# A two-block model kernel on one core: key norms found once, one VectorE operation per state update, decays read one step back

## What is computed

```
kk = heads(k * k_k);  kk = kk * rsqrt(max(sum(kk * kk, per head), 1e-12))
kd = k * (1 + (a - 1) * k_a)                  # a = sigmoid(...), for each direction
S  = S * w_t + (S @ -kk_t) x (kk_t * a_t) + v_t x kd_t      # one step of the scan
y_t = S @ r_t
yn = (y - mean) * rsqrt(var + eps) * lnx_g + lnx_b;  bonus = sum(r * kd * r_k) * v
out = (yn + bonus) * gate
```

## Time and profile before

| | us |
|---|---|
| median of 3 runs | 4076.07 (4070.96 to 4079.86) |
| the profiled execution, its own time | 4080.79 |
| its span in the trace | 4079.0 |
| PE busy | 3704.1 (91%) |
| DVE busy | 2383.0 (58%) |
| ACT busy | 1628.4 (40%) |

### The profile page before, as it was taken

The page is one execution under the profiler, slowest core; times in us unless marked ns, Lnnn a source line. Parts: engine busy times, 40 slices in busy tenths (PEclk is TensorE's granted clock), DMA queues, the critical chain, the costliest instruction groups (busy, mean ns, idle before and its releaser), DMA issues.

```text
span 4079.0 us, 82585 instructions
## 1 busy us (share of the span) xinstructions
PE 3704.1 (91%) x33100; PEld 3370.1 (83%) x33100; DVE 2383.0 (58%) x4281; ACT 1628.4 (40%) x2283; POOL 24.3 (1%) x47
## 2 busy tenths in 40 slices
PE   7999998989899999995999877777778989999998
PEld 5998877779899999994889546666666989999998
DVE  4759995655577775444435437766665444444443
ACT  4545553223455554333123333333231345555333
POOL 0000000000000000000000000000000000000000
PEclk9999998989999999997999987877777999999999
DMA  4547663445355555551234540000000535555553
GB/s 158 175 155 260 248 264 136 155 156 175 134 178 183 184 185 173 181 182 69 93 103 154 189 162 4 5 6 5 5 5 3 185 134 185 185 175 185 179 181 114
DMA packets 80711, 572.00 MB, mean 140 GB/s; under 512 B 9488, under 2 KB 9744, under 8 KB 15472
## 3 DMA queue, kind: packets, MB, share of 16 engines
q1 hardware_dynamic: 78048, 558.50, 39.2%
q0 software_dynamic: 2448, 10.46, 0.8%
HBM read 566.82 MB, written 2.10 MB: 139 GB/s over the span
## 4 chain that ended last, share of the span: by engine, by line
PE 76%; DVE 17%; issue 3%; DMA 2%; ACT 1%; DVEq 0%; SPq 0%; ACTq 0%; POOL 0%
PE po L254 17%; PE po L255 17%; PE po L256 17%; PE po L1424 6%; DVE w_lo L242 2%; PE pa L989 2%; PE po L989 1%; PE pa L300 1%; PE po L418 1%; DMA raw<-ada 1%; DVE s_v L680 1%; PE pa L897 1%; PE po L468 1%; DVE hf L311 1%; PE po L469 1%
## 5 line engine op out<-in xcount | busy, mean ns | idle before, releaser
L242 DVE TENSOR_TENSOR w_lo<-raw,w_hi 128x1024 fp32r<-128x1024 f32 x880 | 1040.5, 1201 | 460.4 <-ACT w_hi L235 443.6
L235 ACT ACTIVATE w_hi<-raw 128x1024 fp32r<-128x1024 f32 (+1 forms) x877 | 898.1, 1038 | 800.8 <-PE po L256 578.3
L254 PE MATMUL po<-hh,w_lo 128*128 128x256 f32 x3744 | 1065.5, 285 | 24.4 <-DVE hh L335 12.6
L255 PE MATMUL po<-hh,w_hi 128*128 128x256 f32 x3744 | 1061.9, 284 | 0.0
L256 PE MATMUL po<-hh,w_hi 128*128 128x256 f32 x3744 | 1061.8, 284 | 0.0
L254 PEld LDWEIGHTS po<-hh,w_lo 128*128 128x128 f32 x3744 | 721.3, 193 | 29.2 <-issue 28.6
L255 PEld LDWEIGHTS po<-hh,w_hi 128*128 128x128 f32 x3744 | 721.4, 193 | 0.3
L256 PEld LDWEIGHTS po<-hh,w_hi 128*128 128x128 f32 x3744 | 721.2, 193 | 0.0
L254 PE MATMUL po<-f_hi,w_lo 128*128 128x256 f32 x1408 | 399.4, 284 | 6.1 <-DVE f_lo L1652 6.1
L255 PE MATMUL po<-f_lo,w_hi 128*128 128x256 f32 x1408 | 399.2, 284 | 0.0
L256 PE MATMUL po<-f_hi,w_hi 128*128 128x256 f32 x1408 | 399.1, 283 | 0.0
(11 more groups left out here) (544 smaller groups left out, 6554.1 us busy)
## 6 DMA issues: line engine op xcount, KB each, us to landing
raw<-ffn_up SPq DMA_DIRECT2D x176, 1024.0 KB, 4.9
raw<-w_in SPq DMA_DIRECT2D x112, 1024.0 KB, 4.9
raw<-ada SPq DMA_DIRECT2D x96, 1024.0 KB, 6.1
raw<-ffn_down SPq DMA_DIRECT2D x64, 1024.0 KB, 4.9
raw<-w_out SPq DMA_DIRECT2D x32, 1024.0 KB, 4.9
raw<-ffn_down SPq DMA_DIRECT2D x32, 768.0 KB, 4.2
raw<-glu SPq DMA_DIRECT2D x16, 1024.0 KB, 6.8
raw<-dn_proj SPq DMA_DIRECT2D x8, 1024.0 KB, 5.3
```

Source lines behind the costliest of these rows:

```text
L235: act.activation(w_hi[:, k % 4, 0:width], raw[:, k // 2 % ring, (k % 2) * PW:(k % 2) * PW + width], ACT.Copy).then_inc(hi_ready, 1)
L242: dve.tensor_tensor(w_lo[:, k % 4, 0:width], raw[:, k // 2 % ring, (k % 2) * PW:(k % 2) * PW + width], w_hi[:, k % 4, 0:width].bitcast(F32 ...
L254: pe.matmul(po[bank][:, 0:T], lo, act_hi[:, t, :], start=first and n == 0, stop=False)
L255: pe.matmul(po[bank][:, 0:T], hi, act_lo[:, t, :], start=False, stop=False)
```

## The change

The inverse of the chunk matrices stays as it is. Six things are edited.

1. Key norms. The per-tile chain for the norm (two DVE operations, matmul with `k_bd`, bound, root, reciprocal, product) goes. Instead, under the last rounds of `w_in2`, ACT squares all keys (eight 128x512 operations), PE sums them with 16 matmuls into rows of one bank (`under_q_pe`), and one bound, one root and one reciprocal of 32x256 are done. In a prep, step 8 spreads two rows over the partitions by one matmul with `k_pick` (filled by ACT in step 1), and one DVE operation makes the keys from it. `first_keys_dve` shrinks in the same way, and clears two banks.
2. State update. `d` is made of four 64x64 blocks on the diagonal instead of two 64x128 matmuls, so that nothing has to be masked; `ks` moves to the other half of the bank. ACT scales the old state into `k_sg` ahead of time, and one DVE operation gives the new state.
3. Shifted decays. `k_gp` (a DVE subtraction and an ACT exponential for each direction) goes; `k_ah` is made from `k_g` one position back, with a small copy for the chunk's edge.
4. `k_vs` and the factor of `kd` move from DVE to ACT (Copy and Identity).
5. The bonus is one addition and one product instead of two products and one addition.
6. In `post`, three DVE operations after the reciprocal become two.

The core of the diff (names of semaphore steps and tile addresses are left out):

```diff
+        NORM_AT = {7 + 2 * j: j for j in range(8)}
+
         def under_q_pe(pe):
             for s in range(32):
+                if s in NORM_AT:
+                    j = NORM_AT[s]
...
+                    pe.wait_ge(*sqa.at(j, "sq"))
+                    for n in range(2):
+                        m = 16 * n + 2 * j
+                        mm = pe.matmul(pa[2][0:32, 0:T], n_sel[:, 32 - m:64 - m], n_sqs[:, j % 2, n * T:n * T + T],
+                                       start=j == 0 and n == 0, stop=j == 7 and n == 1)
+                    mm.then_inc(sqp.did("sum"), 1)
...
         def under_q_act(act):
...
+                    act.activation(n_sqs[:, j % 2, :], zk[:, j, :], ACT.Square, scale=pcol("k_k", j))\
+                       .then_inc(sqa.did("sq"), 1)
+                if s == 25:
+                    act.wait_ge(rows_eps, 1)
+                    act.activation(n_rows[0:32], n_rows[0:32], ACT.Sqrt).then_inc(rows_sqrt, 1)
...
         def under_q_dve(dve):
...
+                    dve.tensor_scalar(n_rows[0:32], pa[2][0:32, 0:T], 1e-12, None, ALU.max).then_inc(rows_eps, 1)
+                if s == 27:
+                    dve.wait_ge(rows_sqrt, 1)
+                    dve.reciprocal(n_rows[0:32], n_rows[0:32]).then_inc(rows_rec, 1)
...
         def prep_pe(pe, j, x, q):
...
-            pe.matmul(I[2][:, 0:T], k_bd[:], k_nrm[:], start=True, stop=True).then_inc(Q.did("sum"), 1)
+            pe.wait_ge(*A.at(j, "pk"))
+            pe.matmul(I[2][:, 0:T], k_pick[0:32], k_rows[0:32], start=True, stop=True).then_inc(Q.did("sum"), 1)
...
         def prep_act(act, j, x, q):
+            act.activation(k_vs[:], zv[:, ds(j, 1), cols_of(x)].rearrange("p a t -> p (a t)"), ACT.Copy)
...
+                    if n:
+                        act.wait_ge(*A.at(j, f"a{e}"))
+                        settle(act)
+                        act.activation(k_kd[e][:], k_a[e][:], ACT.Identity, bias=k_oka[:, ds(j, 1)],
+                                       scale=par[:, ds(j + COL["k_a"], 1)]).then_inc(A.did(f"t{e}"), 1)
+            norm_pick(act, j * 2 + (16 if x == "c" else 2)).then_inc(A.did("pk"), 1)
...
-                act.activation(k_gp[e][:], k_gp[e][:], ACT.Exp, scale=-DECAY).then_inc(A.did(f"gp{e}"), 1)
...
-            act.wait_ge(*V.at(j, "eps"))
-            act.activation(k_nrm[:], k_nrm[:], ACT.Sqrt).then_inc(A.did("sqrt"), 1)
...
         def prep_dve(dve, j, x, q):
-            signal(dve.tensor_copy(k_vs[:], tile(zv)), "vs")
...
-                then(dve.tensor_tensor_scan(b, k_rst[:], s, 0.0, ALU.mult, ALU.add), f"cs{e}")
-                signal(dve.tensor_tensor(k_gp[e][:], k_cs[e][:], k_s[e][:], ALU.subtract), f"sm{e}")
-                dve.wait_ge(*A.at(j, f"a{e}"))
-                then(dve.tensor_scalar(k_kd[e][:], k_a[e][:], 1.0, scale("k_a"), ALU.subtract, ALU.mult), f"t{e}")
-                then(dve.scalar_tensor_tensor(k_kd[e][:], k_kd[e][:], 1.0, tile(zk), ALU.add, ALU.mult), f"kd{e}")
+                signal(dve.tensor_tensor_scan(b, k_rst[:], s, 0.0, ALU.mult, ALU.add), f"cs{e}")
+                dve.wait_ge(*A.at(j, f"t{e}"))
+                then(dve.tensor_tensor(k_kd[e][:], k_kd[e][:], tile(zk), ALU.mult), f"kd{e}")
...
-                signal(dve.tensor_tensor(k_ah[e][:, U], k_kk[:, H], k_gp[e][:], ALU.mult), f"ah{e}")
-                if x == "l":
-                    bo = k_bo if e == 0 else k_x
-                    signal(dve.scalar_tensor_tensor(bo[:], k_kd[e][:], scale("r_k"), zr_j, ALU.mult, ALU.mult), f"bo{e}")
...
+                signal(dve.tensor_copy(ah[:, :, edge], kk[:, :, edge]), f"an{e}")
+                signal(dve.tensor_tensor(ah[:, :, now], kk[:, :, now], g[:, :, ago], ALU.mult), f"ah{e}")
...
-                signal(dve.tensor_tensor(k_bo[:], k_bo[:], k_x[:], ALU.add), "bo2")
+                then(dve.tensor_tensor(k_bo[:], k_kd[0][:], k_kd[1][:], ALU.add), "bo0")
+                signal(dve.scalar_tensor_tensor(k_bo[:], k_bo[:], scale("r_k"), zr_j, ALU.mult, ALU.mult), "bo2")
...
-            then(dve.tensor_scalar(k_kk[:, other], raw_k, kk_col, None, ALU.mult), "kq")
-            signal(dve.tensor_tensor(k_nrm[:], k_kk[:, other], k_kk[:, other], ALU.mult), "sq")
...
-            signal(dve.tensor_scalar(k_nrm[:], I[2][:, 0:T], 1e-12, None, ALU.max), "eps")
+            signal(dve.scalar_tensor_tensor(k_kk[:, other], raw_k, kk_col, I[2][:, 0:T], ALU.mult, ALU.mult), "kk")
...
-            dve.wait_ge(*A.at(j, "sqrt"))
-            then(dve.reciprocal(k_nrm[:], k_nrm[:]), "rec")
-            signal(dve.tensor_tensor(k_kk[:, other], k_kk[:, other], k_nrm[:], ALU.mult), "kk")
...
         def chunk_pe(pe, j, x, q):
...
-                        pe.matmul(X[e][half(c % 2), 0:P], k_ah[e][:, U, c * C:c * C + C], k_S[e][:],
+                        pe.matmul(X[e][half(c % 2), P:2 * P], k_ah[e][:, U, c * C:c * C + C], k_S[e][:],
...
-                        pe.matmul(X[e][:, 0:P], k_bk[e][r, 0, blk, :], k_u[e][r], start=True, stop=False)
-                        mm = pe.matmul(X[e][:, 0:P], k_bk[e][r, 1, blk, :], k_vt[r, blk, :], start=False, stop=True)
+                        settle(pe)
+                        for m, w in enumerate((k_u[e][r], k_vt[r, blk, :])):
+                            for a in range(2):
+                                mm = pe.matmul(X[e][half(a), 64 * a:64 * a + 64], k_bk[e][r, m, blk, half(a)], w[:, half(a)],
+                                               start=m == 0, stop=m == 1)
...
         def chunk_act(act, j, x, q):
...
+                    act.activation(k_sg[e][:], k_S[e][:], ACT.Copy, scale=k_g[e][:, slot(x, q), last:last + 1])\
+                       .then_inc(ch_a[x].did(f"sg{e}_{s}"), 1)
...
         def chunk_dve(dve, j, x, q):
...
-                    dve.scalar_tensor_tensor(out[e][:], X[e][:, 0:P], g, k_bd[:], ALU.mult, ALU.mult)\
-                       .then_inc(V.did(f"sa{e}_{s}"), 1)
...
-                    dve.scalar_tensor_tensor(k_S[e][:], k_S[e][:], g, k_st[e][:], ALU.mult, ALU.add)\
-                       .then_inc(V.did(f"sb{e}_{s}"), 1)
+                    if zero:
+                        dve.tensor_scalar(k_S[e][:], X[e][:, 0:P], g, None, ALU.mult).then_inc(V.did(f"sa{e}_{s}"), 1)
+                    else:
+                        dve.wait_ge(*ch_a[x].at(j, f"sg{e}_{s}"))
+                        dve.scalar_tensor_tensor(k_S[e][:], X[e][:, 0:P], g, k_sg[e][:], ALU.mult, ALU.add)\
+                           .then_inc(V.did(f"sb{e}_{s}"), 1)
...
         def post_dve(dve, j, q):
...
-            then(dve.tensor_tensor(k_y[:], k_y[:], k_ln[:], ALU.mult), "n1")
...
-            then(dve.tensor_scalar(k_y[:], k_y[:], scale("lnx_g"), scale("lnx_b"), ALU.mult, ALU.add), "n2")
-            then(dve.tensor_tensor(k_y[:], k_y[:], k_bv[:, q], ALU.add), "add")
+            then(dve.scalar_tensor_tensor(k_y[:], k_y[:], scale("lnx_g"), k_ln[:], ALU.mult, ALU.mult), "n1")
...
+            then(dve.scalar_tensor_tensor(k_y[:], k_y[:], scale("lnx_b"), k_bv[:, q], ALU.add, ALU.add), "n2")
```

More of the change, by code:

```diff
@@ L1397, in program @@
             + ("" if x == "l" and s == NCH - 1 else "sa0_0 sa1_0" if x == "c" and s == 0
-               else f"sa0_{s} sa1_{s} sb0_{s} sb1_{s}") for s in range(NCH))) for x in "cl"}
+               else f"sb0_{s} sb1_{s}") for s in range(NCH))) for x in "cl"}
         po_p, po_a, po_v = steps("po_p", "mean gate var"), steps("po_a", "y0 gt sq sqrt"), \
-            steps("po_v", "y1 yc eps rec n1 n2 add out")
-        k0a, k0v, k0p = steps("k0_act", "sqrt"), steps("k0_dve", "kq sq eps rec kk"), steps("k0_pe", "sum")
+            steps("po_v", "y1 yc eps rec n1 n2 out")
+        k0v, k0p = steps("k0_dve", "zero kk"), steps("k0_pe", "norm")
+        sqa, sqp = steps("norms_act", "sq"), steps("norms_pe", "sum")
+        sel_set, rows_eps, rows_sqrt, rows_rec = sem("sel_set"), sem("rows_eps"), sem("rows_sqrt"), sem("rows_rec")
+        home = sem("rows_home")
         X, I, inv_bank = (pa[2], po[2]), (pa[0], po[0], pa[1], po[1]), (pa[3], po[3])
@@ L1857, in prep_pe, with norm_pick @@
             yield
+        def norm_pick(act, row):
+            return act.activation(k_pick[0:32].rearrange("p (a c) -> p a c", a=2),
+                                  ident[0:32, ds(row, 2)].unsqueeze(2).broadcast_to([32, 2, 64]), ACT.Copy)
         def prep_act(act, j, x, q):
@@ L2054, in chunk_act @@
             for s in range(NCH):
+                for e in range(2):
+                    if (x == "c" and s == 0) or (x == "l" and s == NCH - 1):
+                        continue
+                    last = order(e)[s] * C + (C - 1 if e == 0 else 0)
+                    if s == 0:
+                        act.wait_ge(*ch_v["c"].at(j, f"sb{e}_{NCH - 1}"))
+                    else:
+                        act.wait_ge(*ch_v[x].at(j, f"sa{e}_0" if x == "c" and s == 1 else f"sb{e}_{s - 1}"))
+                    act.activation(k_sg[e][:], k_S[e][:], ACT.Copy, scale=k_g[e][:, slot(x, q), last:last + 1])\
```

(7 more changed lines are left out.)

91 lines of the change are left out of this document (55 added, 36 removed).

## The result

The changed kernel takes 3963.06 us (median of 4 runs, 3957.27 to 3976.9) against 4075.32 for the kernel before: a ratio of 0.9729, interval 0.9699 to 0.976. 3960 was predicted. The sum came out; its three large terms did not, and that their errors cancel to within 3 us is luck. The profiled execution after took 3957.27 us, its span is 3955.6.

What follows compares the result with a forecast made beforehand. It took the recurrent branch as bound by a chain passing between PE and DVE, plus clock falls after idle stretches. 77 (seven tiles at 11.0) + 17 (fill, tail) - 7 (sums) + 29 (clock) = 116 us off 4076: 3960, range 3912 to 4022.

Steps and rivals of the forecast that it cites:

- waits shortened: Per tile: joins 3.0, prep steps 3.6, state update 2.0, rest 0.7 us won, less 0.8 for marks and delayed post work.
- The joins and the prep steps: Joins of halves: c to l 2.0, l to c 1.0 us a tile; prep steps 2 and 3: 3.6 together.
- `d` matmuls ... together 2.5: Four 64x64 blocks save 0.25 us a step, 0.5 at half clock: l half 1.5, c half 1.0 a tile.
- The clock. With the joins shortened ..., 29: Shorter idle at joins lets the clock hold in slow stretches behind them: 58 us for seven tiles, half taken, 29.
- Rival B: Clock holds at both joins and falls at prep steps get rarer: 87 + 58 + 10 won, 3921 us; chance 0.20.
- The Trainium skill's drain: Table switch ahead of k_gi: skill says 2.66 us with drain; prediction took none, k_gi starting 1.30 after the load began.
- Rival D: Small d blocks don't pay, loads and matmuls run in a row: 1.35 us more a step, 4131 us; chance 0.03.
- Rival C: Saving becomes waits on ACT's chain and PE's slow matmuls, clock unchanged, a third of 94 us hidden: 4020; chance 0.24.
- The signs: Profile after: tile 73 to 75 us, clock above 0.79, k_ur and state waits halved or less, d steps 0.4.
- Fill and tail: Outside the seven full tiles: first keys 3, two preps ahead of tile 0 9, tile 7 5; together 17 us won.
- the sums: Norm sums under w_in2, where PE is the bound: 16 matmuls at 0.43 us, nothing hides them, 7 us cost.

Runs made afterwards that it cites:

- d_full: The changed kernel with each d step as two full 64x128 matmuls again and no mask; 3994.44 us, 31 more than the changed kernel.
- old_keys: The kernel before with only the key norms changed (sums under w_in2, pick matmul); 4052.84 us, ratio 0.9935.
- recip_back: The changed kernel with an unused reciprocal of the same size put back where the norm's stood; 4002.84 us, 40 more.
- recip_filled: The changed kernel with the unused reciprocal put back and with matmuls that nothing reads for an idle TensorE; 3960.83 us.
- late_root: The changed kernel with post's root and reciprocal moved to turns of their own, on ScalarE and VectorE; 3938.23 us, 25 less.

## Why the prediction came out, point by point

Over the thirteen halves of the table the change wins 573.6 - 469.7 = 103.9 us. It divides so: idle time 33.3; the `d` blocks 26.0 (d_full); slow time 116 us less, at 0.37 each 43; 1.7 is left. The prediction, at 6.5 tiles:

| term | predicted | measured |
|---|---|---|
| waits shortened (3.0 + 3.6 + 2.0 + 0.7 - 0.8 a tile) | 55 | 33 |
| `d` blocks (2.5 a tile) | 16 | 26 |
| clock (29 for seven) | 27 | 43 |
| left over | | 2 |
| sum | 98 | 104 |

The measured column comes from two profiled executions that lie 123.5 us apart, while the medians lie 112.3 apart: one was above its median, the other below. At the median the clock term is smaller. The changed kernel's runs have some 428 us at 0.50 in all against the 411 of the profiled one, which is 6 us at the price above.

- **The joins and the prep steps** were priced rightly one by one: 1.56 us from `d` to `u` against 1.35, 1.16 won at prep step 2 against 1.1, and the idle time that each part takes away alone is 22.6, 12.2 and 17.5, together 52 against 49 for these terms. What failed is the addition: "Sum for a tile: ... 11.0 us, with every stretch at the clock that it has now". With all three in, only 33 us of idle time go. What fits is that TensorE, quicker by blocks and clock, reaches VectorE's next result earlier and waits again. The wait for `k_ur` is still 37.2 us, not half.
- **"`d` matmuls ... together 2.5"** is a mis-sized term: 4.0. The larger error is in the l half: 1.5 a tile was priced and 16.5 / 6 = 2.8 measured. The sum there has four steps ("0.5 twice ..., 0.25 twice") where the l half has six, and it prices a block by its own duration, though the second direction's blocks run beside the first one's outputs. The c half's 1.0 came to 9.5 / 7 = 1.4.
- **"The clock. With the joins shortened ..., 29"** had the right sign and the right place, but shortening the joins is not enough to bring it about. The heads of the halves are now nearly all fast, and the falls at the prep steps, which the prediction left in, have stayed. But old_keys, with the norm's tail taken out of the joins, gave no slow time back. The other parts alone gave 9 and 36 us, and all together 116, which is 43 us and not 27. That the clock counts at all, and costs more than the wait that brings it, is shown by recip_back and recip_filled. Rival B's clock (58 + 10 for seven tiles, 63 at 6.5) wasn't reached.
- **The Trainium skill's drain** ("ScalarE: Activation LUTs", "What ACT_TABLE_LOAD costs"): `k_gi` starts 1.30 us after its table load began, in this kernel too (2737.59, 2738.89). No drain is seen, and the term of 1.1 us that hung on it was had.
- **Rival D**, and the Trainium skill's rule behind it ("TensorE: Matmul & The Clock Gate", "Part 3: Packing small matmuls"): the four blocks of one direction, all in one row half, take 0.38 us and not 2.0, and d_full is 31 us slower than the blocks, so the price that the prediction drew from the rule isn't paid here. The blocks that run beside the other direction's outputs stand in the other row half, since the two directions go through the chunks in opposite order.
- **Rival C** had a third of the branch's saving turn into another wait. Something like it happened: 22 of the 55 us of shortened waits are missing. But its road, ScalarE's `k_gi`, is a wait of 6.7 us in all; the longest waits of TensorE are still for VectorE.
- **The signs.** The tile (72.8), its clock, the `d` steps (0.38) and the wait for the state came as stated. The wait for `k_ur` fell to two thirds and not to half, `u` starts 1.56 us and not 1.5 behind `d`, and the stretch under `w_in2` is 9.4 us longer and not 7. The prediction also misread the page's clock row by one: its low slices are 24 to 31.
- **Fill and tail, and the sums.** From the landing of the first keys' data to tile 0's first prep matmul it is 53.5 us (2429.67 to 2483.17) instead of 60.3 (2423.24 to 2483.50): 6.7 won and not 3 + 9. Of these, 1.2 lie ahead of the first scan; the pick matmul alone takes 1.19 at half clock. The last three halves, to tile 7's `post` reciprocal, take 87.2 us instead of 106.2: 19 won and not 13 (5.5 for half a tile, 2 of the clock, 5 for tile 7). The sums cost 9.4 and not 7. These errors cancel too. The 3 us that are left of the 123.5 lie in stretches that the change doesn't touch.

Left open is what decides whether an idle stretch of TensorE is followed by 0.50 (last section). That it also sets the spread of the runs is in their clocks: the changed kernel's four runs took 3957.27, 3957.67, 3976.9 and 3968.45 us at mean clocks of 0.948, 0.949, 0.942 and 0.944. The third has 54 us more at 0.50 than the first two (461 and 407) and is 19.4 longer, 0.36 a microsecond, the same price as above.

## What to carry to other kernels

In a chain that passes between engines, read TensorE's busy time, its idle time and its time at 0.50 for every version, since a saving in one moves the others. Price waits one by one, but don't add them up: here three parts took 52 us of idle time apart and 33 together. Where TensorE stands idle for a microsecond or two again and again, matmuls into spare PSUM are a cheap test of what its clock is worth: they won 32 us in the kernel before, 16 in the changed one and 15 in late_root, and made the difference between 40 and 13 us for the same reciprocal.
